# A hybrid decoder step on one Trainium2 core: low-rank rows in other buffers, weight sums by a new timetable, and the recurrence's keys turned in another bank

## The reference

```python
h = rms_norm(x, ln_w)
proj = jnp.einsum('bsd,de->bse', h, w_in)                 # 1024 -> 8720 columns
aq, ak, av, az, gq, gk, gv, gz, glr, mg_a, mg_b = jnp.split(proj, splits, axis=-1)
aq = partial_rope(...) * HEAD_DIM ** -0.5                  # 24 heads of 64; keys likewise
gate_pre = einsum('bsr,rk->bsk', glr, w_gla_a2) + b_gla_a  # rank 16 -> 256
log_a = log_sigmoid(gate_pre) / 16                         # per key column of 4 heads
```

```python
def step(state, inp):
    q_, k_, v_, b_ = inp                       # b_ = running sum of log_a in the chunk
    qe, ke = q_ * exp(b_), k_ * exp(-b_)
    att = where(causal, einsum('bhtk,bhsk->bhts', qe, ke), 0)
    o = att @ v_ + einsum('bhtk,bhkv->bhtv', qe, state)
    kd = k_ * exp(b_last - b_)                 # the keys that the change is about
    return exp(b_last) * state + einsum('bhsk,bhsv->bhkv', kd, v_), o
```

## Time and profile before

| | |
|---|---|
| median of 3 runs | 2405.78 us (2403.83 to 2407.98) |
| the profiled execution | 2415.95 us |
| its span in the profile | 2414.2 us, so 1.75 us lie around it |
| busy: PE / DVE / ACT / POOL | 2279.2 / 1708.3 / 806.2 / 277.2 us |
| granted TensorE clock, mean | 0.979 of full speed |
| DMA moved | 553.40 MB, mean 229 GB/s |

### The profile page before, as it was taken

How to read it: one execution, slowest core, us unless ns; L and a number is a source line. 1 busy time by engine, 2 the same in 40 slices (tenths; PEclk the granted TensorE clock), 3 DMA queues, 4 the chain that set the end, 5 groups by cost and what they waited for, 6 DMA issues and landing times. The chain is left out here.

```text
span 2414.2 us, 36166 instructions
## 1 busy us (share of the span) xinstructions
PE 2279.2 (94%) x12996; PEld 1839.5 (76%) x12996; DVE 1708.3 (71%) x3345; ACT 806.2 (33%) x1705; POOL 277.2 (11%) x455
## 2 busy tenths in 40 slices
PE   6999999987999999999999998889899897999998
PEld 4887878866788888888878886667777646888887
DVE  5855767856775688888868886778888757655653
ACT  4332221112223422222122233676767524122221
POOL 1000011221210012212121220001010010000000
PEclk8999999998999999999999999899999999999999
DMA  8999999999996666888787797665555398434431
GB/s 255 244 278 319 274 287 276 254 248 244 298 268 213 202 197 225 271 257 265 253 249 241 250 322 262 216 211 191 174 194 170 113 293 327 160 128 170 154 148 70
DMA packets 271184, 553.40 MB, mean 229 GB/s; under 512 B 33392, under 2 KB 60480, under 8 KB 268896
## 3 DMA queue, kind: packets, MB, share of 16 engines
q1 hardware_dynamic: 200688, 358.77, 44.1%
q0 software_dynamic: 58000, 166.36, 26.5%
q10 hardware_dynamic: 12320, 25.96, 2.8%
HBM read 442.60 MB, written 191.50 MB: 263 GB/s over the span
## 5 line engine op out<-in xcount | busy, mean ns | idle before, releaser
L1633 PE MATMUL b_acc<-b_whi,a_hi 128*128 128x512 f32 x1792 | 706.4, 394 | 28.5 <-ACT b_u L1062 15.1
L1635 PE MATMUL b_acc<-b_whi,a_lo 128*128 128x512 f32 x1792 | 701.3, 391 | 0.0
L1634 PE MATMUL b_acc<-b_wlo,a_hi 128*128 128x512 f32 x1792 | 701.2, 391 | 0.0
L1633 PEld LDWEIGHTS b_acc<-b_whi,a_hi 128*128 128x128 f32 x1792 | 338.7, 189 | 101.3 <-ACT b_u L1062 15.5
L1045 ACT CAST b_whi<-b_w 128x2048 fp32r<-128x2048 f32 (+1 forms) x127 | 228.6, 1801 | 546.3 <-PE b_acc L1635 380.8
L1635 PEld LDWEIGHTS b_acc<-b_whi,a_lo 128*128 128x128 f32 x1792 | 338.5, 189 | 71.5
L1634 PEld LDWEIGHTS b_acc<-b_wlo,a_hi 128*128 128x128 f32 x1792 | 338.8, 189 | 68.9
L1295 DVE TENSOR_TENSOR b_wlo<-b_w,b_whi 128x2048 fp32r<-128x2048 f32 (+1 forms) x127 | 273.1, 2151 | 83.1 <-ACT b_whi L1045 82.9
L1089 ACT ACTIVATE c_sm<-c_sm,c_ends 128x256 f32<-128x256 f32 (+1 forms) x384 | 172.4, 453 | 9.5 <-DVE c_ends L1436 9.5
L1436 DVE CUSTOM_DVE_ANT_0 c_sm<-c_p_s,c_mask 128x256 f32<-128x256 f32 (+1 forms) x384 | 117.1, 361 | 39.3 <-PE c_p_s L1722 38.6
L970 POOL DMA_DIRECT2D a_x<-tm x188 | 107.2, 574 | 285.9 <-DVE sT L1402 217.5
(11 more groups left out here) (373 smaller groups left out, 3477.3 us busy)
## 6 DMA issues: line engine op xcount, KB each, us to landing
b_w<-t SPq DMA_DIRECT2D x64, 1024.0 KB, 8.1
t<-in_w_in POOLq DMA_DIRECT2D x48, 1024.0 KB, 10.9
b_w<-in_w_in SPq DMA_DIRECT2D x47, 1024.0 KB, 8.0
a_x<-tm POOLq DMA_DIRECT2D x167, 256.0 KB, 6.8
tm<-b_st SPq DMA_DIRECT2D x128, 256.0 KB, 7.0
b_ck<-in_cache_kv_w POOLq DMA_DIRECT2D x96, 256.0 KB, 5.1
c_qk<-tm SPq DMA_DIRECT2D x96, 256.0 KB, 3.6
t<-t POOLq DMA_DIRECT2D x16, 1024.0 KB, 12.3
```

The costliest lines, as they stand in the source:

```text
L1633: nc.tensor.matmul(out, stat_hi, mov_hi, start=first, stop=False)
L1634: nc.tensor.matmul(out, stat_hi, mov_lo, start=False, stop=False)
L1635: return nc.tensor.matmul(out, stat_lo, mov_hi, start=False, stop=last)
```

## The change

There are seven edits.

1. *Low-rank rows.* The low-rank turns' results go into `ub[2+p]` and `stb[2]` in place of `ub[p]` and `nb`, and their evacuations wait for the stores of the turn before the last one instead of the last.
2. *Weight sums.* A new timetable `sums_at`. For turn 7 the steps go to slots 145, 151, 157, 163 and 169. They were spread over the fm turn and the low-rank turn. Those of turn 5 are 3 slots apart.
3. *Conversions ahead of splits.* In a slot of the projection, ACT and DVE do the conversion of turned tokens before the weight split. In the first turn the split of a block of four slots comes one slot later, two `scale`s come a slot earlier, POOL starts its sums on the first x tile in place of the second, and SP's loads of x tiles 5 to 8 wait for the first two copies of the sums.
4. *Second half's tokens.* `pair_begin` is spaced by 18 slots in place of 16, the last sums come two slots later, and the first of the two stores of scaled tiles is issued a slot earlier, after the first tile.
5. *Items.* The 72 early ones start 8 slots later and end where they did.
6. *Gate rows.* `load_recurrence` and the first `load_rank` go from slots NSLOT+2 to NSLOT-4 and NSLOT-3.
7. *Keys.* The turn of kd goes from `c_p_qk` at t+3 to the output part of `c_p_g` at t+1, with a semaphore of its own, its copy on ACT from t+3 to t+2, and `within` waits for that copy instead of `scaled_g`.

The diff, cut to its core:

```diff
@@ tables
-            split_at[blocks[b - 1][2] + (2 if b == 1 else 1)] = b
+            split_at[blocks[b - 1][2] + (2 if blocks[b - 1][3] - blocks[b - 1][2] == NPAIRS else 1)] = b
-    for s, what, n in ((0, "scale", 2), (1, "stat", 2), (1, "scale", 3), (2, "scale", 4), (3, "stat", 3)):
+    for s, what, n in ((-1, "scale", 2), (1, "stat", 2), (1, "scale", 3), (1, "scale", 4), (3, "stat", 3)):
-    pair_begin = [turns[1].begin + 2 + 16 * p for p in range(NPAIRS)]
+    pair_begin = [turns[1].begin + 2 + 18 * p for p in range(NPAIRS)]
-            add_prep(s + 11, form, 1, p)
+            add_prep(s + 13, form, 1, p)
-    early_from, early_to = turns[3].begin + 6, tail - 8
+    early_from, early_to = turns[3].begin + 14, tail - 8
-            since = turns[turn.n - 2 if turns[turn.n - 1].kind == "glr" else turn.n - 1]
-            at = since.begin + (8 if turn.n == 1 else 1)
+            at, step = turns[turn.n - 1].begin + 1, (turn.begin - turns[turn.n - 1].begin) // 6
+            if turn.n == 1:
+                at, step = at + 7, 4
+            elif turn.kind == "fm":
+                step = 3
+            elif turns[turn.n - 1].kind == "glr":
+                at, step = turns[turn.n - 3].begin + 17, 6
             for k in range(5):
-                sums_at.setdefault(at + k * (turn.begin - at) // 6, []).append((turn.n, k))
+                sums_at.setdefault(at + k * step, []).append((turn.n, k))
-    for n, at in t_at.items():
-        turn_qk_at[at + 3] = (n, 3)
@@ SP
                 def store_scaled(p):
-                    sp.wait_ge(scaled, prep_no["scale", odd(1, p)])
+                    sp.wait_ge(scaled, prep_no["scale", even(1, p)])
                     sp.dma_start(XT[p, 0:2, :, :].rearrange("a t e -> t a e"), ...).then_inc(xt_out, 16)
+                    sp.wait_ge(scaled, prep_no["scale", odd(1, p)])
                     sp.dma_start(XT[p, 2, :, :], xs[:, 1, CH:]).then_inc(xt_out, 16)
-                rank_at = {max(NSLOT + 2, q // 2 - 4): k for k, q in g_at.items()}
+                rank_at = {q // 2 - 4 if k else NSLOT - 3: k for k, q in g_at.items()}
-                scaled_at, summed_at = {s + 7: p ...}, {s + 13: p ...}
+                scaled_at, summed_at = {s + 6: p ...}, {s + 15: p ...}
-                for i in range(4, 9):
+                load_x(4)
+                sp.wait_ge(t_in, 32)
+                for i in range(5, 9):
                     load_x(i)
+                    if s == NSLOT - 4:
+                        sp.wait_ge(scored, N_IT)
+                        sp.wait_ge(roped_, len(rope_no))
+                        sp.wait_ge(sq_act, len(norm_no))
+                        load_recurrence()
                     if s == NSLOT + 2:
                         project_over(sp)
-                        load_recurrence()
@@ POOL
-                pool.wait_ge(x_in[1], 16)
+                pool.wait_ge(x_in[0], 16)
@@ ACT
                     if x.kind == "glr":
-                        group_free(act, x, UU)
-                        nc.scalar.copy(ub[0:2 * RANK, x.p, :], bank[0:2 * RANK, :]).then_inc(act_ev, 1)
+                        act.wait_ge(stored[UU], 16 * group_end[x.turn - 2][UU])
+                        nc.scalar.copy(ub[0:2 * RANK, 2 + x.p, :], bank[0:2 * RANK, :]).then_inc(act_ev, 1)
                 def kd_evac(n):
-                    act.wait_ge(tqk_done, tqk_no[n, 3])
+                    act.wait_ge(kd_turned, n + 1)
-                    nc.scalar.copy(kdT[:, :, :], p_qk[:, 0:NP * P]...).then_inc(kd_evacd, 1)
+                    nc.scalar.copy(kdT[:, :, :], p_kd).then_inc(kd_evacd, 1)
-                    if q - 3 in tile_of:
-                        kd_evac(tile_of[q - 3])
+                    if q - 2 in tile_of:
+                        kd_evac(tile_of[q - 2])
@@ DVE (ACT's split_hi moves in the same way)
-                        if s in split_at:
-                            split_lo(split_at[s])
                         for c in conv_at.get(s - 1, ())[2 * (s == 1):] if s else ():
                             conv(c)
+                        if s in split_at:
+                            split_lo(split_at[s])
@@ PE
-                    if a == 3:
-                        pe.wait_ge(scaled_g, i + 1)
-                        for c in range(NP):
-                            last = nc.tensor.transpose(p_qk[:, c * P:(c + 1) * P], ge[1][:, c, tile_cols(i)], ident[:, :])
+                def turn_keys(n):
+                    pe.wait_ge(scaled_g, n + 1)
+                    if n >= 1:
+                        pe.wait_ge(go_evacd, n)
+                    for c in range(NP):
+                        last = nc.tensor.transpose(p_kd[:, c, :], ge[1][:, c, tile_cols(n)], ident[:, :])
+                    last.then_inc(kd_turned, 1)
                 def within(n):
-                    pe.wait_ge(scaled_g, n + 1)
+                    pe.wait_ge(kd_evacd, n + 1)
                 def recur(q):
+                    if q - 1 in tile_of:
+                        turn_keys(tile_of[q - 1])
```

More of the change, by code:

```diff
@@ L448, in project @@
         turn_qk_at[units[4 * i].q + 9] = (i, 2)
-    for n, at in t_at.items():
-        turn_qk_at[at + 3] = (n, 3)
-    assert len(turn_qk_at) == 3 * N_TASK + NT
+    assert len(turn_qk_at) == 3 * N_TASK
     tqk_no = {turn_qk_at[at]: n + 1 for n, at in enumerate(sorted(turn_qk_at))}
-    turned_first = {what: [sum(1 for i, a in tqk_no if a == kind and tqk_no[i, a] < n) for kind in range(4)]
+    turned_first = {what: [sum(1 for i, a in tqk_no if a == kind and tqk_no[i, a] < n) for kind in range(3)]
                     for what, n in tqk_no.items()}
@@ L1318, in evac_new @@
                         return
+                    if x.phase is None:
+                        y = stb[0:NS, 2, :]
+                        dve.wait_ge(stored[ST], 16 * group_end[x.turn - 2][ST])
+                        V.tensor_tensor(y[:, 0:w], bank[:, 0:w], nb[NS:P, 0:w], ALU.add).then_inc(dve_ev, 1)
+                        dve.wait_ge(dve_ev, dve_no[s] - 1)
+                        V.tensor_tensor(y[:, 0:RANK], y[:, 0:RANK], y[:, RANK:2 * RANK], ALU.add).then_inc(dve_ev, 1)
+                        return
                     if x.phase == Q3:
@@ L1342, in evac @@
                         group_free(dve, x, ST)
+                        if turns[x.turn - 1].kind == "glr":
+                            group_free(dve, x, NEWS)
                         V.tensor_tensor(st_, bank, v_, ALU.add).then_inc(dve_ev, 1)
@@ L1588, in _ @@
                     if s < NSLOT:
+                        for c in conv_at.get(s - 1, ())[2 * (s == 1):] if s else ():
+                            conv(c)
                         if s in split_at:
                             split_lo(split_at[s])
-                        for c in conv_at.get(s - 1, ())[2 * (s == 1):] if s else ():
-                            conv(c)
                         prepare(s)
@@ L1685, in transposes @@
                 def transposes(i, a):
-                    for done, n in zip((q_evacd, k_evacd, o_moved, kd_evacd), turned_first[i, a]):
+                    for done, n in zip((q_evacd, k_evacd, o_moved), turned_first[i, a]):
                         if n:
@@ L1690, in transposes @@
                         pe.wait_ge(h_dve, N_CONV)
[L1691 to L1702 removed]
+                    if a < 2:
+                        pe.wait_ge(qk_in[i % 2], 32 * (i // 2) + 32)
+                    else:
+                        pe.wait_ge(o_evacd, i + 1)
+                    for c in range(4):
+                        y = oT[:, c, :] if a == 2 else qk[:, i % 4, a, c * P:(c + 1) * P]
+                        last = nc.tensor.transpose(p_qk[:, c * P:(c + 1) * P], y, ident[:, :])
                     last.then_inc(tqk_done, 1)
```

26 lines of the change are left out of this document (9 added, 17 removed).

## The result

The change made the kernel slower: 2459.14 us, the median of 4 runs (2452.36 to 2461.46), against 2405.48 us before (4 runs). The ratio is 1.0217 (95% interval 1.0199 to 1.0235), so 2.0 to 2.4% slower. I had forecast 2407, with 2379 to 2427 as the range.

A forecast was written before the change was run, and what follows sets the result against it. PE was busy 2279.2 of 2414.2 us, so only stretches where it stands still could be won. Gains of 46 us less losses of 47.5 made 1.5 slower than 2405.78: 2407.3 us, range 2379 to 2427.

The forecast's parts named there:

- The keys' turn: Recurrence tiles: PE newly waits for the scaled keys and for their copy before `within`; a loss of 41.1 us.
- The rival of a cheap turn: Recurrence: the exps are not held by PE's delay, cost 18.1 us and no clock, total 2379.4; chance 0.22.
- that of no cost: Recurrence: the 10.5 us of PE's waits go and no new ones come, total 2351; chance 0.10.
- The clock: Recurrence: low PE clock after the gaps before `within`, 0 to 27 us possible, 5 taken as loss.
- over half of each hidden: Recurrence: over half of each low-clock cost goes unseen because PE then waits for ACT anyway; used in taking 5 us.
- the clock falls at every tile: Recurrence: gaps before `within` bring the low clock each time, 27 us instead of 5, total 2429; chance 0.15.
- Low-rank rows: Projection, at 566.71 us: PE's 15.07 us wait for ACT's copy and the low clock behind it go; gain 16 us.
- Turn 5's weights: Projection, turn 5: earlier weight sums cut PE's waits for splits and one on `b_nb`; gain 7 us, bounds 3 and 12.
- Start: Projection's first turn: PE's 10.22 us wait for a scaling goes, 3 us of wait stay; gain 8.5 us.
- Second half's tokens: Projection, at 226.19 us: PE's 5.25 us wait for DVE and a second on `b_nb` go; gain 9 us.
- Gates: Gates' start after the projection: earlier low-rank rows cut PE's 9.47 us wait, memsets still late; gain 5.5 us.
- Items: Projection, round 650 us: 72 items over 127 slots instead of 135, denser on DVE and DMA; loss 1.5 us.
- the DMA engines keep the projection's gaps: Projection: moved sums only move the queue, turns 5 and 7 gain less, items cost more; 15.5 us worse, 2423; chance 0.13.

The follow-up runs named there:

- keys_alone: The kernel before with only the turn of the keys moved, with its copy and the wait of `within`; 2461.7 us, ratio 1.0237.
- copy_first: The changed kernel with ACT's copy of the keys one step earlier, ahead of the exps; 2402.4 us, 0.9978 of the kernel before.
- keys_undone: The changed kernel with the keys' turn, its copy and the wait of `within` put back as before; 2397.2 us, 0.9963 of the kernel before.
- gates_alone: The kernel before with only the gate rows and constants loaded before the projection's end; ratio 0.9984.
- start_alone: The kernel before with only the first turn's edits (scalings sooner, split later, POOL's sums on first x tile, SP's loads behind first copies); ratio 1.0001.
- rank_alone: The kernel before with only the low-rank results in the other buffers; ratio 0.9999.
- rank_light: The kernel before with low-rank results in the other buffers and 72 early query loads cut to a quarter, making some scores wrong; ratio 0.9959.

## Why the prediction was wrong

*The keys' turn* was right in mechanism, place and waits: 41.1 us forecast, 42.0 measured (37.0 + 15.5 - 10.5). The list of what the profile would show had 46 us of waits in all, which does not fit the sum's 41.1 + 10.5; 52.5 were measured. The rival of a cheap turn (18.1) and that of no cost fell.

*The clock* was mis-sized: 5 us taken, 11 to 20 measured (11.4 and 15.9 left over in the stage's length in two profiled executions, 0.94 against 0.97 over 400 us in keys_alone, 57 us for removing 37.0 in copy_first). That half of the gaps bring the low clock was right, nearly: 9 and 10 of 16. The step that failed is "over half of each hidden": 11.4 of 15 us and 15.9 of 17 were paid. PE's late work is what ACT's next exps wait for, which I take as the reason; no run shows that by itself. The rival "the clock falls at every tile" (27) was about as far off on the other side, and its condition did not come true. The Trainium skill, TensorE: Matmul & The Clock Gate, section "HAM oscillation", describes a loop in which the clock falls in every round and is paid for in every round; its waits are longer than these. The runs here show it in 9 and 10 of 16 rounds for gaps of 2.0 to 2.5 us, and in none for those of 0.7 to 1.2 us in copy_first.

*The projection* is where the sum failed. It had 8.5 + 9 + 7 + 16 - 1.5 = 39 us of gains. keys_undone, which has all of them and the gates, is 0.4% faster, 9 us (5 to 13 by the interval), of which the gates alone give 4. So about 5 us, where 39 were forecast. By step:

- "The 10.17 us between them I put to the execution as a whole and to no term." They were in the projection, where the terms were read. The wait on `b_u` was 15.07 us in that execution, and 11.9, 8.9 and 8.7 in others with the same buffers (keys_alone, gates_alone, start_alone); the projection of keys_alone ended 10 us sooner on the same instructions, and that of gates_alone 4.
- *Low-rank rows*: "What is late next is the weight of turn 7, whose sums now come sooner. Gain 16". This is the largest term that failed. The thing next was misnamed and its price taken as 0.8 us. Alone the edit gave 0.0%: in rank_alone DVE stood 14.26 us for an item's query at the same place, ahead of the split in its list, with the weight long converted. With the sums moved that wait moved with them, to 3.7 us of PE's in turn 4 of the changed kernel, and turns 4 and 5 together became 15 us longer. The prediction counts the items only as traffic and not as instructions that the splits stand behind.
- "*Turn 5's weights*: I take 7." The sign of the waits was wrong: those on `b_wlo` rose from 7.6 to 20.3 us. I had read the DMA share of 0.96 in turn 4 and still counted the moved transfers there as free. The formula cited there (the Trainium skill, DMA: Bandwidth & Descriptors, section "Anatomy of one DMA") is given for transfers that GpSimd issues, and SP issued this load, so the 3.2 us was a rough guide at best.
- "*Start*: 8.5." In place 3.7 us, in time nothing. From 150 to 640 us the DMA engines' share was 0.87 to 1.06 in every stretch read, and what PE gained ahead of that was lost inside it.
- "*Second half's tokens*: 9" went the same way: the wait at 226 us is gone, turn 2 is 5.9 us shorter, and turn 3 gives 2.2 back at once. The edit was not run alone.
- "*Gates*: 5.5." Measured 4, with an interval of 0.2 to 7.5. PE's 9.47 us are gone, and the waits for masks (`c_ends`) grew from 9.9 to 15.5.
- "*Items*: a loss of 1.5" was not run alone.

The rival "the DMA engines keep the projection's gaps" was the nearest, and its price of 15.5 us was too small by half: it should have taken all of the terms and not three. It had the weights as what is late, too, where at turn 7 it was an item's load. Together the clock with 6 to 15 us, the projection with 34, the keys with 1 and the gates with 1.5 make 43 to 52 of the 52 us between 2407 and 2459.

## What to carry to other kernels

Before a stall is counted as a gain, look for the second thing that is late at the same place, and look for it in the whole list of the engine that PE waits for: a wait named after a split was DVE standing for an item's load, a few instructions ahead. Where the DMA engines' share was 0.9 and more, four kernels here that each took a wait away gained nothing (0.9999 to 1.0017), and 13 MB less traffic gave 9 to 16 us. A turn or a copy that is moved "ahead" in an in-order list is ahead only if its input is ready there: put it behind work that covers its producer, and its copy ahead of the long work that doesn't need it. And take the spread of a stall from more than one execution before its size goes into a sum.

## What the runs showed of the hardware

Sixteen gaps of PE of 2.0 to 2.5 us cost 11 to 20 us more than their length. Behind 9 and 10 of them the granted clock was 0.70 to 0.74 over 5.7 us, behind the others 1.00, and gaps of the same length stand on both sides. Sixteen of 0.7 to 1.2 us (copy_first) were all followed by 1.00. The lowest mean clock of any kernel here, 0.973, is that of the profiled execution of keys_alone, and runs of the changed kernel between 0.974 and 0.981 differed by up to 9 us.

A 256 KB load that POOL issued behind two transfers of 1 MB took 19 us until DVE could use it, at a DMA share of 1.09 (rank_alone, issued at 534.90, used at 553.78); one of a quarter of the size, at the same place in rank_light and at a share of 1.10, took 18.
